# First loads of five stages moved into the stage ahead of each, and two dense pieces placed between the halves of the first scores

## What is computed

```python
h   = x * (1 + scale_m) + shift_m                # x = input LayerNorm; scale, shift from c @ w_ada
p   = h @ w_in                                   # RWKV-7 r,k,v,lora | attention q,k,v | two gates
A   = RWKV-7 time mixing                         # chunked delta-rule scan
B   = sliding-window attention (128), sinks      # prompt: banded blocks; samples: cache of 128 rows
mix = (sigmoid(gate_a) * (A @ w_pa) + sigmoid(gate_b) * (B @ w_pb)) @ w_o
x   = LN(alpha * x + gate_m * mix)
q   = h2 @ peer_wq;  s1, s2 = q against two key tables of 128; top 16 of each, top 16 of their sums
ff  = sum over 8 heads x 16 picks of  gate * gelu(u[idx] . h2) * v[idx]     # 16384 experts
x   = LN(alpha * x + gate_f * ff)
```

## Time and profile before

| | us |
|---|---|
| median of 3 runs | 4104.53 (4103.16 to 4109.38) |
| the profiled execution, its own time | 4102.66 |
| its span, first to last instruction | 4100.8 |
| PE busy | 3521.2 (86%) |
| DVE busy | 2378.0 (58%) |
| POOL busy | 1410.7 (34%) |
| ACT busy | 1093.0 (27%) |
| mean granted TensorE clock | 0.927 of full speed |
| moved by DMA | 973.75 MB, mean 237 GB/s |

### The profile page before, as it was taken

One profiled execution on the slowest core, in us unless ns is written; L12 is line 12 of the kernel. 1 busy time (PEld: TensorE's weight loads), 2 busy tenths in 40 slices (PEclk: granted clock), 3 DMA queues, 4 the chain that ended last, 5 costly groups with the idle time before them and its releaser, 6 DMA issues. The chain is left out here.

```text
span 4100.8 us, 58646 instructions
## 1 busy us (share of the span) xinstructions
PE 3521.2 (86%) x22506; PEld 2538.4 (62%) x22506; DVE 2378.0 (58%) x4792; ACT 1093.0 (27%) x1919; POOL 1410.7 (34%) x1269
## 2 busy tenths in 40 slices
PE   5998999997879998988899999886787788778996
PEld 3666767673656887766676666664554455555565
DVE  3364222225223432999979988985666666664445
ACT  2121111111322232322263455344111111112222
POOL 0001111110002011244454545453666566665540
PEclk8999999997769999999999999998999899989998
DMA  5101110015115124688899999889999999999992
GB/s 196 36 31 38 32 34 28 30 36 194 64 36 206 42 89 136 233 289 292 285 394 352 333 371 378 332 328 349 396 378 385 366 397 394 396 393 394 390 370 75
DMA packets 367057, 973.75 MB, mean 237 GB/s; under 512 B 35937, under 2 KB 133417, under 8 KB 359872
## 3 DMA queue, kind: packets, MB, share of 16 engines
q0 software_dynamic: 150912, 549.52, 35.1%
q1 hardware_dynamic: 215872, 420.45, 29.0%
HBM read 863.29 MB, written 106.55 MB: 237 GB/s over the span
## 5 line engine op out<-in xcount | busy, mean ns | idle before, releaser
L2055 POOL DMA_INDIRECT u_rows<-in_u_rows,idx_u x512 | 635.8, 1242 | 883.4 <-DVE dots L2093 700.4
L2093 DVE CUSTOM_DVE_ANT_0 u_rows<-u_rows,x_rows 128x1024 f32<-128x1024 f32 x512 | 620.1, 1222 | 125.6 <-DMA u_rows<-in_u_rows,idx_u 104.7
L2066 POOL DMA_INDIRECT v_rows<-in_v,idx_v x512 | 588.4, 1149 | 247.4 <-issue 141.8
L2521 PE MATMUL hid_ps<-dh,u_high 128*128 128x512 f32 x1152 | 476.0, 413 | 82.4 <-DVE u_low L2778 59.8
L2521 PE MATMUL hid_ps<-dl,u_high 128*128 128x512 f32 x1152 | 471.4, 409 | 0.0
L2521 PE MATMUL hid_ps<-dh,u_low 128*128 128x512 f32 x1152 | 469.2, 407 | 0.0
L2984 ACT ACTIVATE dh<-v_raw 128x1024 fp32r<-128x1024 f32 x128 | 135.4, 1058 | 730.4 <-DMA v_raw<-in_v 573.6
L2152 PE MATMUL ff_ps<-v_rows,diag 128*8 128x512 f32 x2048 | 262.5, 633 | 67.7 <-DMA v_rows<-in_v,idx_v 62.2
L2521 PEld LDWEIGHTS hid_ps<-dh,u_high 128*128 128x128 f32 x1152 | 225.2, 195 | 149.3 <-DVE u_low L2778 82.4
L3039 PE MATMUL turn_ps<-w_high,dh 128*128 128x512 f32 x384 | 173.0, 450 | 152.4 <-DVEq L3121 121.8
L687 PE MATMUL side_ps_scan<-h,w_side_scan 128*128 128x344 f32 x768 | 270.3, 478 | 1.5 <-DMA w_side_scan<-in_w_side 0.9
(11 more groups left out here) (458 smaller groups left out, 6538.6 us busy)
## 6 DMA issues: line engine op xcount, KB each, us to landing
u_raw<-in_u SPq DMA_DIRECT2D x128, 512.0 KB, 6.2
v_raw<-in_v SPq DMA_DIRECT2D x128, 512.0 KB, 11.3
hidden_saved<-hid SPq DMA_DIRECT2D x128, 256.0 KB, 6.5
gates_saved<-gates SPq DMA_DIRECT2D x32, 1024.0 KB, 8.5
hidden_back<-hidden_saved SPq DMA_DIRECT2D x128, 256.0 KB, 13.4
g_back<-gates_saved SPq DMA_DIRECT2D x60, 320.0 KB, 14.1
g_back<-gates_saved SPq DMA_DIRECT2D x30, 384.0 KB, 20.4
side_saved<-side_scan SPq DMA_DIRECT2D x16, 516.0 KB
```

Source lines behind the costliest of these rows:

```text
L2055: self.nc.gpsimd.indirect_dma_start(self.u[:, n % RU], None, self.io["u_rows"], bass.IndirectOffsetOnAxis(ap=index, axis=axis)).then_inc(l ...
L2066: self.nc.gpsimd.indirect_dma_start(self.v[:, n % RV], None, self.io["v"], bass.IndirectOffsetOnAxis(ap=index, axis=0)).then_inc(self.v_la ...
L2093: V.tensor_tensor_reduce(self.u[:, n % RU], self.u[:, n % RU], self.xt[:], 1.0, 0.0, ALU.mult, ALU.add, accum_out=self.dots[:, i % 2, k:k ...
L2521: mm = nc.tensor.matmul(ps[b % 2][:], u[:, b % RING, k], h[:, k], start=at == 0, stop=at == 3 * KD - 1)
```

## The change

1. **w_in**: the ring `w` gets a fixed place at the top of the memory (W_IN_AT), and its first three blocks are asked for in modulation_and_input, after the w_ada blocks and ahead of the stores of x. SP no longer waits for those stores at the stage's end; ACT and POOL do at the start of rwkv_inputs.
2. **Cache**: kc, vc and rel are asked for at the start of attention, behind the biases.
3. **merge**: w_merge and gate for m = 0, 1 are asked for at the start of the samples' block, ahead of its three stores; x and the eight blocks of w_o behind those stores.
4. **peer_up**: keys and the first two u_raw blocks are asked for in output_and_queries once PE has done with w_o; the first half of the first queries at query block 11. Two pieces of beat 0 (16 matmuls) now stand between the two halves of the first scores.
5. **peer_down**: hidden_back and v_raw for rows 0 and 1, then the first gates in six cuts, are asked for at the end of peer_up, behind its last store of hidden values.

New semaphores hold these arrivals: ten more calls of `sems`, two at the start of the program, three ahead of attention, two ahead of output_and_queries, three ahead of peer_up. Five of the ten are given the stack that ends ahead of peer_up, five the stacks that end with the program. `sm` in the samples' block and in merge has seven semaphores fewer in all. No arithmetic changes.

```diff
@@ modulation_and_input
                 for n in range(2 * NT, ADA_FIRST):
                     ada.load(sp, io, n)
+                for n in range(3):
+                    sp.dma_start(w[:, n], io["w_in"][n]).then_inc(w_loaded[n], 16)
                 for t in range(NT):
...
-                sp.wait_ge(x_stored, 16 * NT)
@@ rwkv_inputs
-                for n in range(3):
-                    load(n)
                 sp.dma_start(before[:], io["shift_before"]).then_inc(small_loaded, 16)
...
+                act.wait_ge(x_stored, 16 * NT)
...
+                pool.wait_ge(x_stored, 16 * NT)
@@ attention, second block
-                    sp.dma_start(kc[:], io["k_cache"]).then_inc(loaded, 16)
-                    sp.dma_start(vc[:], io["v_cache"]).then_inc(loaded, 16)
-                    sp.dma_start(rel[:], io["sample_bias"]).then_inc(loaded, 16)
-                    sp.wait_ge(loaded, 49)
+                    for m in range(2):
+                        early.load(sp, io, m)
+                    sp.wait_ge(loaded, 48)
                     sp.dma_start(io["v_win_sample_out"][0:WIN - 1], vc[1:WIN]).then_inc(kv_stored, 16)
...
                     sp.dma_start(io["k_win_sample_out"], kw[:]).then_inc(kv_stored, 16)
+                    sp.dma_start(x[:], io["x_saved"]).then_inc(early.x_back, 16)
+                    for n in range(KD):
+                        sp.dma_start(wo_raw[:, n], io["w_o"][n]).then_inc(early.wo_loaded, 16)
                     sp.wait_ge(kv_stored, 49)
@@ output_and_queries
+                sp.wait_ge(o_summed, len(TILES) * KD)
+                sp.dma_start(start.keys[:], io["keys"]).then_inc(start.keys_loaded, 16)
+                for b in range(2):
+                    sp.dma_start(start.raw[:, b], io["peer_wq"][b]).then_inc(start.u_loaded[b], 16)
                 for n in range(COUNT):
+                    if n == NH + 3:
+                        for s in range(2):
+                            sp.wait_ge(q_stored[s], 16 * (NH // 2))
+                        sp.dma_start(start.qt[:], io["query_saved"][0:NH, :, 0:P].rearrange("j p n -> p j n")).then_inc(start.q_loaded, 16)
@@ plan_up
-    out += [("rows", 0), ("load_u", 0), ("load_u", 1), ("split_u", 0), ("low_u", 0), ("query", 0, 0), ("scores", 0, 0),
-            ("query", 0, 1), ("scores", 0, 1), ("load_u", 2), ("split_u", 1), ("low_u", 1)]
+    out += [("rows", 0), ("split_u", 0), ("low_u", 0), ("scores", 0, 0), ("query", 0, 1), ("load_u", 2), ("split_u", 1), ("low_u", 1)]
+    for at in (0.0, QUICK):
+        pieces(at)
+    out.append(("scores", 0, 1))
@@ peer_up, SP
+                def gates_back(stored):
+                    nonlocal cuts
+                    while room_free and cuts < GCUTS and Ahead.blocks(cuts).stop <= stored:
+                        b = Ahead.blocks(cuts)
+                        for n in (b.stop - 2, b.stop - 1):
+                            sp.wait_ge(g_stored[n % 2], 16 * (n // 2 + 1))
+                        sp.dma_start(ahead.g[:, 0, b], io["gates"][:, b, 0:GLOAD]).then_inc(ahead.g_loaded[0], 16)
+                        cuts += 1
...
+                        if b == BEATS - 1:
+                            room_free = True
+                            for c in range(2):
+                                sp.wait_ge(h_stored[c % 2], 16 * ((NQ + c) // 2 + 1))
+                                sp.dma_start(ahead.hid[:, c], io["hidden_saved"][c]).then_inc(ahead.h_loaded[c], 16)
+                                sp.dma_start(ahead.v_raw[:, c], io["v"][c * NKEY:(c + 1) * NKEY]).then_inc(ahead.v_loaded[c], 16)
```

More of the change, by code:

```diff
@@ L1554, in _, with merge @@
                         step(V.tensor_tensor(ob[r, :, TP:T].rearrange("p c b -> p b c"), part[r, :, kv], o_ps[r, :, kv], ALU.add))
-def merge(nc, io, sb, pb, sm, x, wo_raw, ya, ob, mh, ml, **_):
+def merge(nc, io, sb, pb, sm, x, ya, ob, mh, ml, early, **_):
     SETS = 4
     with ExitStack() as ph:
-        w = sb(ph, "w_merge", [P, 2, 2, NP, P])
-        gate = sb(ph, "gate", [P, 2, 2, T])
+        sb(ph, "merge_room", [P, 4 * NP * P + 4 * T])
+        assert nc.sbuf_base == early.end
+        w, gate, w_loaded, g_loaded, x_back = early.w, early.gate, early.w_loaded, early.g_loaded, early.x_back
         part = sb(ph, "merge_part", [P, 2, 2, TN])
@@ L2330, in plan_up @@
     piece = 0
+    last_at = None
     horizon = 0.0
     def pieces(now):
-        nonlocal pe, piece
+        nonlocal pe, piece, last_at
+        if piece == BEATS * PIECES and last_at is not None and now > last_at + 2 * PIECE:
+            out.append(("finish_u", BEATS - 1))
+            last_at = None
         while pe <= now and piece < BEATS * PIECES:
@@ L2394, in plan_up, with __init__, blocks, peer_up @@
     pieces(1e9)
-    out.append(("finish_u", BEATS - 1))
+    if ("finish_u", BEATS - 1) not in out:
+        out.append(("finish_u", BEATS - 1))
     feed.now = now
     return out
-def peer_up(nc, io, sb, pb, sems, consts, dh, dl, sparse, feed, **_):
+GLOAD = 8
+GWAIT = 2
+GCUTS = GLOAD - GWAIT
+class Ahead:
+    SIZE = 2 * D + 2 * TDN + 2 * TDN * GLOAD
+    def __init__(self, nc, sems, ph):
+        self.at = -(-nc.sbuf_base // 32) * 32
+        at = nc.alloc_sbuf_tensor_at
+        self.v_raw = at("v_raw", [P, 2, D], F32, offset=self.at)
+        self.hid = at("hidden_back", [P, 2, TDN], F32, offset=self.at + 8 * D)
+        self.g = at("g_back", [P, 2, TDN // GS, GLOAD, GS], F32, offset=self.at + 8 * D + 8 * TDN)
+        self.v_loaded = sems(ph, "v0_loaded", "v1_loaded")
+        self.h_loaded = sems(ph, "h0_loaded", "h1_loaded")
+        self.g_loaded = sems(ph, "g0_loaded", "g1_loaded")
+    @staticmethod
+    def blocks(cut):
+        return slice(cut * (TDN // GS) // GCUTS, (cut + 1) * (TDN // GS) // GCUTS)
+def peer_up(nc, io, sb, pb, sems, consts, dh, dl, sparse, feed, ahead, start, **_):
     order = plan_up(feed)
@@ L2408, in peer_up @@
     with ExitStack() as ph:
-        raw = sb(ph, "u_raw", [P, 2, KD, P])
+        raw, keys, qt = start.raw, start.keys, start.qt
         uh = sb(ph, "u_high", [P, RING, KD, P], F32R)
@@ L2867, in plan_down, with peer_down @@
     return out
-def peer_down(nc, io, sb, pb, sems, consts, vecs, mod, dh, dl, sparse, feed, **_):
+def peer_down(nc, io, sb, pb, sems, consts, vecs, mod, dh, dl, sparse, feed, ahead, start, **_):
     order = plan_down(feed)
```

156 lines of the change are left out of this document (90 added, 66 removed).

## The result

The changed kernel takes **4091.91 us** (median of 19 runs), the kernel before 4106.62 on the same chip; the ratio is 0.997 with an interval of 0.9962 to 0.9978. In a later job they took 4090.09 (6 runs) and 4105.43 (17), ratio 0.9962 (0.9948 to 0.9976). So the change is worth about 15 us by the medians, and 12 and 16 us by the two ratios. The profiled run took 4094.46, its span is 4092.5; before it was 4100.8.

The account below looks back on a forecast made before the run. The prediction took peer_up as bound by DVE and PE, peer_down by transfers. Terms -3.7 - 0.8 + 5.5 - 11.5 - 3 = -13.5 took 4102.66 to 4089.2; adding 1.9 for the median gave 4091.0 us, range 4079 to 4100.

Parts of the forecast that it names:

- Step 1: w_in: PE's wait for w and SP's end wait for stores go; -3.7 us.
- Step 2: Samples and merge: early loads delay the one-engine store by 3 us, leaving -0.8 us of the naive -8.6.
- Step 3: Barriers and clearings between stages: ten more barriers and added clearings, nothing hidden; +5.5 us.
- Step 4: Start of peer_up: early loads let DVE's selection start sooner; -11.5 us, bounds -9.7 and -15.5.
- Step 5: peer_up to peer_down: x_sparse asked for earlier, though the stage and POOL's gathers start later; -3 us.
- The rival in which peer_up gives the gain back: peer_up: gathers, stores and loads hold the pace, a third of the start's gain left; 4098.7 us, chance 0.18.
- the slow one: End of peer_up: six gate cuts hold SP up to 50 us, peer_down opens late; 4130 us, chance 0.05.
- first rival: Samples' store not held, or PE's lead carries through peer_up; 4084.7 or 4087 us, chance 0.15.

Follow-up runs that it names:

- loads_last: The changed kernel with the early merge loads asked for behind all three stores of the samples' block; 4092.67 us in its single run.
- before_split: The kernel before with only its 127-partition store cut into 112 and 15 partitions; 4098.02 us, ratio 0.9979.
- pieces_back: The changed kernel with the two dense pieces behind both halves of the first scores again, all early loads kept; 4101.47 us, ratio 0.9975.
- store_split: The changed kernel with the 127-partition store of the value cache cut into 112 and 15 partitions; 4089.81 us, ratio 0.9953.
- no_ahead: The changed kernel with hidden rows, v rows and first gates asked for in peer_down again, gates as one ask; 4092.34 us, ratio 0.9966.

## Why the prediction was right, and where its terms were not

4091.0 was forecast, 4091.91 measured, with 12 to 16 us of gain where I had 13.5. The agreement is better than the terms deserve: to within a microsecond it is luck.

- **Step 1, -3.7.** The length fell by 3.9 in all eleven profiles of kernels with it. Right, by its own steps.
- **Step 2, -0.8.** 34.3 became 33.9 and 34.0: -0.3. The step behind it, that the trickle starts 3 us later and takes the gain, is what the rate shows, and the order of work on one engine is shown by loads_last. What I had not followed through is that it is the k cache's store that counts, so that moving the store to the front helps by 1 us only, and that SP itself stands for 20 us inside two asks.
- **Step 3, +5.5.** The direct price is smaller: 0.6 from the last asks of w_ada to attention (19.25 on average in the seven profiles with the separate calls, against 18.69 in before and before_split), 1.3 in mid (355.9 against 354.6, the same profiles) and 0.9 at the end, 2.8 in all: I took the spacing of the barriers' rows for their price, and it is about twice that. But the three barriers ahead of attention also cost 2.7 us inside it, by the longer stretch at half clock. The sum, 5.5, is right for a reason that I did not have.
- **Step 4, -11.5.** At MAX8 just that: 10.8 to 11.8 us after the opening, where it was 23.0 to 23.3 in the three kernels without early loads. But the stage's length fell by more: 1211.3 on average in ten profiles against 1222.2, 1228.3 and 1231.1, mean 1227.2. That is -15.9, on my bound of -15.5, with some 4 us of scatter on each side. The step that failed is the choice "I stay near DVE's number since DVE is the fuller engine": TensorE's pieces began 15.8 us sooner, and in the one profile of pieces_back the end moved with them. No run undoes the early loads of step 4 while keeping the new place of the pieces.
- **Step 5, -3.** Measured +2, within the stage's scatter of none. SP's last gate cut ended at 2807.48 + 7.52 = 2815.0 and the stage opened at 2816.2, 12.5 us after the last store; the forecast had 12.9. The times of its chain were right (first product 4.1 us sooner, TensorE 5.9 sooner), and so was x_sparse, 3 us sooner. What failed is the inference from x_sparse's ask to the end of the stage: a third of the way in, 0.7 us of lead were left, and the wait for `ff_back` was 2.4 us longer.

The mean lengths sum to -3.9 - 0.3 + 5.5 - 15.9 + 2.2 = -12.4, and the scatter of the two long stages alone, some 4 us each way, is larger than what separates this from 13.5 or 15. The rival in which peer_up gives the gain back is out, as *up* shows; so is the slow one, since the six gate cuts held SP for 7.5 us together, not for 32. Of the first rival one half came true (step 4 at its bound), and was paid for by step 5.

The two best kernels, with the store cut and the barriers drawn together, take 4073 us with step 5 and 4072 and 4078 without it, 26 to 34 under the kernel before: about twice the change as it was made. Not all of this is the two edits: the stretch ahead of attention, whose work nobody changed, took 927.5 and 923.6 us in the two profiles of the one without step 5, 3 to 11 less than in all others.

## What to carry to other kernels

Before loads are put ahead of a stage's end, look at what the stage's last wait really waits for: here it was half a megabyte on one DMA engine, and cutting a 127-partition store into 112 and 15 brought 14 us at a border where three megabytes of earlier loads brought 0.3, and the loads were worth 6.8 only once the store was cut. When a start is moved on two engines by different amounts, let an experiment say which of them sets the pace; the fuller one late in the stage need not be it early on. And ask for semaphores in one call per object: a barrier cost about 0.17 us here, and three of them 2.7 us more by where they shifted the work.

## What the runs showed of the hardware that was not expected

- **Tenths of a microsecond can move 2.7.** Three idle barriers ahead of attention lengthen it from 38.3 to 41.0 us between two stores, in each of the eight profiles of kernels that have them or their like, because TensorE then does 10.2 us of that work at half clock in place of 3.4.
- **SP can stand for ten microseconds inside one ask.** An ask of 1 MB for all engines stood 9.64 us behind 508 KB on one engine, and eight asks of 512 KB stood 9.2 to 12.4 us with or without such a store in front. That a queue was full is the likely reason; no view shows the queue.
- **A stall that changes its size.** Near a third of peer_down TensorE and VectorE stand still for `ff_back`, while the transfers run on at 371 to 402 GB/s (store_split, 3210 to 3220 us); then the rate drops to 31 GB/s for 5 us. TensorE waits 5.6 us in before, 9.0 in changed, 7.9 in no_ahead, and in store_split:

```profile
PE turn_ps L3156 <- DMA ff_back<-ff_rows: 12.1, 1, 12.1
```

  Over the fourteen profiles the wait goes from 5.6 to 12.3 us and down from 1272.6 to 1279.7. Less the wait, down is 1265.2 to 1269.6, so most of the scatter of *down* is this one wait.
